# Expert search on VectorE: 2048-column sums and combinations in two pieces of 1024 columns

## What is computed

```python
def peer_ffn(h, w_q, sub1, sub2, u, v):
    qry = (h @ w_q).reshape(B, S, 8, 256)
    s1 = jnp.einsum('bshd,hkd->bshk', qry[..., :128], sub1)     # 128 keys a head
    s2 = jnp.einsum('bshd,hkd->bshk', qry[..., 128:], sub2)
    v1, i1 = lax.top_k(s1, 16)
    v2, i2 = lax.top_k(s2, 16)
    cand = (v1[..., :, None] + v2[..., None, :]).reshape(B, S, 8, 256)
    cand_idx = (i1[..., :, None] * 128 + i2[..., None, :]).reshape(B, S, 8, 256)
    top_s, pos = lax.top_k(cand, 16)
    expert = jnp.take_along_axis(cand_idx, pos, axis=-1)
    gate = jax.nn.softmax(top_s, axis=-1)
    a = jnp.einsum('cd,ced->ce', x_c, u[e_c])
    ...
    return jnp.einsum('ce,ced->cd', gelu(a) * gate, v[e_c])
```

## Time and profile before

| | |
|---|---|
| median of 3 runs | 1931.25 us (1930.73 to 1932.47) |
| the profiled execution | 1932.39 us, its span 1930.7 us |
| share of the span in which an engine is busy | PE 98%, DVE 78%, ACT 60%, POOL 12% |
| the search on VectorE | 209.78 to 314.24 us of the span |
| granted TensorE clock | 1.00 in every stretch read here (2.4 GHz) |

### The profile page before, as it was taken

How to read it: one execution, slowest core, us unless ns; L and a number is a source line. 1 busy time by engine, 2 the same in 40 slices (tenths; PEclk the granted TensorE clock), 3 DMA queues, 4 the chain that set the end, 5 groups by cost and what they waited for, 6 DMA issues and landing times.

```text
span 1930.7 us, 38686 instructions
## 1 busy us (share of the span) xinstructions
PE 1899.4 (98%) x12752; PEld 1728.6 (90%) x12752; DVE 1501.1 (78%) x3609; ACT 1157.9 (60%) x2442; POOL 233.6 (12%) x262
## 2 busy tenths in 40 slices
PE   9899999999999999999999999999999999999998
PEld 8779999999888899999989898998889989998886
DVE  6676798888778878888888487877887568887776
ACT  5645666998444444544466577655557567765555
POOL 1000695665000000000000000010000000010000
PEclk9999999999999999999999999999999999999999
DMA  8446555444775588777757533565665553455552
GB/s 309 153 171 236 179 174 169 139 150 137 255 254 192 198 312 288 280 281 291 263 206 262 197 131 121 171 212 191 248 246 177 186 175 121 139 179 175 185 191 103
DMA packets 109463, 388.33 MB, mean 201 GB/s; under 512 B 12160, under 2 KB 16528, under 8 KB 108304
## 3 DMA queue, kind: packets, MB, share of 16 engines
q1 hardware_dynamic: 95040, 335.40, 50.6%
q10 hardware_dynamic: 8096, 28.70, 4.3%
q0 software_dynamic: 6192, 22.55, 3.2%
HBM read 379.76 MB, written 6.82 MB: 200 GB/s over the span
## 4 chain that ended last, share of the span: by engine, by line
PE 86%; DVE 9%; ACT 2%; DVEq 2%; issue 1%; DMA 0%; ACTq 0%; SPq 0%
PE bank L763 13%; PE bank L771 12%; PE bank L768 12%; PE bank L1002 7%; PE bank L1008 7%; PE bank L1005 7%; PE bank L1405 5%; PE bank L1069 3%; PE bank L1402 2%; PE bank L901 1%; PE bank L1214 1%; DVE part_lo L2159 1%; PE bank L1263 1%; ACT part_hi L1473 1%; DVE arena L2388 1%
## 5 line engine op out<-in xcount | busy, mean ns | idle before, releaser
L1473 ACT ACTIVATE part_hi<-ring 128x512 fp32r<-128x512 f32 x1124 | 692.0, 626 | 369.8 <-PE bank L768 162.6
L2159 DVE TENSOR_TENSOR part_lo<-ring,part_hi 128x512 fp32r<-128x512 f32 (+1 forms) x764 | 507.6, 685 | 158.0 <-ACT part_hi L1473 148.8
L763 PE MATMUL bank<-u_hi,part_hi 128*128 128x256 f32 (+1 forms) x1888 | 545.2, 289 | 4.9 <-POOL part_lo L2061 3.4
L771 PE MATMUL bank<-u_hi,part_lo 128*128 128x256 f32 (+1 forms) x1888 | 529.8, 281 | 0.0
L768 PE MATMUL bank<-u_lo,part_hi 128*128 128x256 f32 x1808 | 505.8, 280 | 0.0
L763 PEld LDWEIGHTS bank<-u_hi,part_hi 128*128 128x128 f32 (+1 forms) x1888 | 354.7, 188 | 13.2 <-POOL part_lo L2061 4.6
L771 PEld LDWEIGHTS bank<-u_hi,part_lo 128*128 128x128 f32 (+1 forms) x1888 | 356.8, 189 | 0.0
L768 PEld LDWEIGHTS bank<-u_lo,part_hi 128*128 128x128 f32 x1808 | 339.7, 188 | 3.1
L1002 PE MATMUL bank<-part_hi,w_hi 128*128 128x512 f32 x688 | 269.1, 391 | 0.2 <-DVE w_lo L2488 0.2
L1008 PE MATMUL bank<-part_lo,w_hi 128*128 128x512 f32 x688 | 268.0, 389 | 0.0
L1005 PE MATMUL bank<-part_hi,w_lo 128*128 128x512 f32 x688 | 267.9, 389 | 0.0
(11 more groups left out here) (354 smaller groups left out, 3223.5 us busy)
## 6 DMA issues: line engine op xcount, KB each, us to landing
ring<-stream_dram SPq DMA_DIRECT2D x606, 512.0 KB, 3.3
arena<-ada_dram ACTq DMA_DIRECT2D x54, 512.0 KB, 4.7
arena<-ada_dram POOLq DMA_DIRECT2D x42, 512.0 KB, 4.5
acts_kept<-act SPq DMA_DIRECT2D x32, 128.0 KB, 3.6
arena<-acts_kept SPq DMA_DIRECT2D x4, 1024.0 KB, 5.4
xT<-x_dram SPq DMA_DIRECT2D x4, 256.0 KB, 5.4
arena<-mem_dram SPq DMA_DIRECT2D x1, 1024.0 KB, 9.1
arena<-keys_dram SPq DMA_DIRECT2D x1, 1024.0 KB, 8.2
```

The source lines that it names most:

```text
L763: m = pe.matmul(o, hi, u(cc), start=first, stop=False)
L771: m = pe.matmul(o, lo, u(cc), start=False, stop=last)
L1473: act.activation(part_hi[:, h % 4, 0:width], ring[:, n % RING, (h % 2) * width:(h % 2 + 1) * width], ACT.Copy).then_inc(hi_ready, 1)
L2159: v.tensor_tensor(part_lo[:, h % 4, 0:width], ring[:, n % RING, (h % 2) * width:(h % 2 + 1) * width], part_hi[:, h % 4, 0:width], ALU.subt ...
```

## The change

The sum into `cand` is made for heads 0 to 3 and then for heads 4 to 7, 1024 columns each. The combination into `apart` and the minimum behind it are made for the first four heads and then for the last four, so that the order on VectorE is combination, drain, minimum, combination, drain, minimum, drain for each side and tile. Nothing else is altered: the values, the buffers and the waits between engines stay.

```diff
-                v.tensor_tensor(cnd,
-                                topv[:, tt, 0:8, :].unsqueeze(3).to_broadcast([P, 8, 16, 16]),
-                                topv[:, tt, 8:16, :].unsqueeze(2).to_broadcast([P, 8, 16, 16]), ALU.add)
+                for h in (0, 4):
+                    v.tensor_tensor(cnd[:, h:h + 4, :, :],
+                                    topv[:, tt, h:h + 4, :].unsqueeze(3).to_broadcast([P, 4, 16, 16]),
+                                    topv[:, tt, 8 + h:12 + h, :].unsqueeze(2).to_broadcast([P, 4, 16, 16]), ALU.add)
...
                     at = at.bitcast(U32)[:, tt, :].rearrange("p (h k) -> p h k", h=8)
-                    v.tensor_tensor(apart_u.rearrange("p (h k a) -> p h k a", h=8, a=16),
-                                    at.unsqueeze(3).to_broadcast([P, 8, 16, 16]),
-                                    placed.bitcast(U32)[:, tt, side * 8:side * 8 + 8, :].unsqueeze(2)
-                                    .to_broadcast([P, 8, 16, 16]), ALU.bitwise_xor)
-                    v.drain()
-                    v.tensor_reduce(picks[:, side, tt, :], apart_u.rearrange("p (k a) -> p k a", a=16), AX_X, ALU.min)
+                    spread = apart_u.rearrange("p (h k a) -> p h k a", h=8, a=16)
+                    for h in (0, 4):
+                        v.tensor_tensor(spread[:, h:h + 4, :, :],
+                                        at[:, h:h + 4, :].unsqueeze(3).to_broadcast([P, 4, 16, 16]),
+                                        placed.bitcast(U32)[:, tt, side * 8 + h:side * 8 + h + 4, :].unsqueeze(2)
+                                        .to_broadcast([P, 4, 16, 16]), ALU.bitwise_xor)
+                        v.drain()
+                        v.tensor_reduce(picks[:, side, tt, h * 16:h * 16 + 64],
+                                        apart_u[:, h * 256:h * 256 + 1024].rearrange("p (k a) -> p k a", a=16),
+                                        AX_X, ALU.min)
                     v.drain()
```

## The result

| | before | changed |
|---|---|---|
| median of 8 runs each | 1931.55 us (1930.73 to 1932.47) | 1937.74 us (1936.70 to 1939.33) |
| ratio to before | | 1.0032, 95% interval 1.0021 to 1.0042 |
| the profiled execution, and its span | 1932.39, 1930.7 us | 1937.62, 1935.9 us |
| search on VectorE | 209.78 to 314.23 | 209.48 to 317.94 |
| start of the last L1069 matmul, the end of the dense stage | 478.52 | 483.51 |

The changed kernel is slower by 6.2 us. The forecast was 1935.2 us with a range of 1932.3 to 1936.9, so the result lies 0.8 us above the upper end of the range. Of the 2.5 us to the forecast, 0.3 are the median of the kernel before, which came out at 1931.55 and not at 1931.25.

A forecast was written before the change was run, and what follows sets the result against it. TensorE, 98% busy, bounds the kernel, and VectorE's end of the search decides when it resumes. First tile +3.57 and second +0.30 gave +3.87, taken as +3.95 us: median 1935.2 us, range 1932.3 to 1936.9.

The forecast's parts named there:

- what bounds the end: Behind the search TensorE has no idle time, so delay of VectorE's search end, 314.24, moves the end one for one.
- the fixed cost: On VectorE's list, two split sums at 0.08 and four split combinations with minima at 0.29 add 1.32 us.
- the waits, one by one: Walk through VectorE's waits for GpSimd's rests: with fixed cost, first tile 3.57 us later, second tile +0.30.
- The margin of 0.11 us: Next combination arrives 1.21 us behind the last one's end, GpSimd's second rest starts at 1.10, so it waits.
- rival (1): Rests fit under the minima, all eight combination waits zero, second sums still wait 1.08: +0.42 us, 1931.7 us; 12%.
- (2): Walk holds in kind but loses two or three first-tile waits: +1.3 to +3.3 us, 1932.6 to 1934.6; 14%.
- (3): Only two-port modes block; combinations keep their waits for another reason: +1.32 us, 1932.6 us; 2%.
- (4): GpSimd's last rest comes later than about 309.5, second tile's last three combinations wait: +7.9 at most, 1939.2; 14% over +4.7.
- (5): VectorE and GpSimd fall in step, all 8.87 us of waits go, TensorE gives back 3.9 us: 1927.4 us; 2%.
- the last one of the sum: Search ends at 318.2, TensorE resumes at 319.2 after standing since about 311.4; all behind moves by the same, +3.95 us.
- The sign: Whole kernel against the 0.2% line, 3.9 us: slower 48%, within it 50%, faster 2%.

The follow-up runs named there:

- the two quiet kernels: GpSimd's rests cut to 16 of 512 columns, in the kernel before and in the changed kernel; 1927.91 and 1927.47 us, one execution each.
- more_rests_pieces: Changed kernel with GpSimd making the rests of 37 experts instead of 34 and the gate's exponentials two experts later; median 1937.83 us against 1932.16 before.
- the third execution: The changed kernel once more, since an edit meant to add matmuls was void; median 1938.18 us against 1932.78 before.
- warm_filled: Changed kernel with TensorE's experts 30 to 35 written out and 56 unread matmuls before half 68; median 1936.61 us against 1932.16 before.
- sums_only: Kernel before with only the sums into `cand` in two pieces, combinations and minima whole; median 1934.91 us against 1932.78 before.
- quiet_whole: Kernel before with GpSimd's rests cut to 16 of 512 columns, other columns left out; 1927.91 us, one execution.
- quiet_pieces: Changed kernel with GpSimd's rests cut to 16 of 512 columns, other columns left out; 1927.47 us, one execution.
- comb_quarters: Kernel before with combinations and minima in four pieces of 512 columns, sums whole; 1938.67 us, one execution.

## Why the prediction was wrong by 2.5 us, point by point

**Right: what bounds the end.** The figure to forecast was the search's end, and a delay there was handed on to the end (the stages behind took only 0.24 us more). TensorE takes up half 68 at 0.98 us behind it in both kernels, and GpSimd's last rest, 4.9 us earlier, bought nothing.

**Right: the fixed cost.** 1.32 us by the sum, 1.36 us by the two quiet kernels.

**Right: the waits, one by one.** The second sum of each tile 1.08 and 1.09 (1.08 forecast), L2407 unchanged, the copy of the first tile 0 (0), the first tile's combinations 0.95, 1.05, 0.90, 1.06 (0.94, 1.04, 0.89, 1.04), the last three of the second tile 0 (0). The copy of the second tile waited 1.06 where 0.95 was forecast. GpSimd's last rest ran from 306.74 to 308.12 (306.9 to 308.3). The search grew by 4.01 us where +3.95 was forecast, and each half of the change gave its share, 1.18 and 2.82. The margin of 0.11 us is seen in a row: the second combination arrives at 253.66, 0.10 behind the start of the second rest at 253.56. At 512 columns it arrives under the first rest and waits 0.33. No run puts a combination just ahead of a rest, so what rival (1) would have given was not seen.

**The rivals.** (1) and (2), pieces that find the port free, fell: every combination that followed another one waited, in all kernels where GpSimd had work. (3), only two-port modes block, fell with the quiet kernels. The Trainium skill, "Advanced Engine Details and Errata", section "VectorE Performance Modes", names no other modes; the prediction's "by that page" is too wide, since it holds for this section and not for the whole page. The uint32 combination of 3.35 us that falls to 2.29 when GpSimd's rests are short speaks against the rule. (4), a late last rest, did not occur here, and more_rests_pieces shows what it would have cost the search: 7.0 us more than before, where the prediction had 7.9 at most for the time. (5), all waits gone, fell.

**The step that failed** is the last one of the sum: "TensorE resumes at 319.2, having stood since about 311.4, and all behind it moves by the same amount". The halt was forecast, from 311.4 to 319.2, and it came, from 311.35 to 318.92. What I did not read off my own forecast is that TensorE comes back from such a halt at half its clock. In the stretch that I read, its longest halt before was 1.27 us and the clock column read 1.00 throughout, so I took the pace behind the search, for given. The 7.57 us of halt brought it to 0.50, and the matmuls behind it cost 0.214 instead of 0.118 us, 17 of them in one execution, 28 in another kernel's. 17 x 0.096 is 1.6 us, of which the profiled execution gives 0.3 back, because a short wait of the kernel before (a matmul that starts at 318.36, 0.2 late, and the one behind it, 0.1 late) is gone; in the third execution 2.1 us remain. 4.0 + 1.3 to 2.1 is 5.3 to 6.1, and the medians are +6.2, +5.7 and +5.4. warm_filled takes that term away alone: with TensorE kept busy, the sum is again the forecast's (+4.05 in the trace, +4.45 by the medians). No row of before shows TensorE behind a halt of 7 us, so its cost was an unknown to be bounded: from nothing to half pace for as long as the halt, which is half of 7.6 us, would have put the upper end at 1935.2 + 3.8 = 1939.0 instead of 1936.9. That is a guess that would have served here and no rule: in sums_only the low stretch of the work, 6.1 us, was longer than the halt of 3.77.

**The sign.** My forecast lay on the 0.2% line, and the missing term decided: slower, for which I had 0.48.

## What to carry to other kernels

Where two engines hold each other up, as VectorE's combinations and GpSimd's rests did here, a cut instruction meets the other engine anew with each piece, as long as that one has work queued. What counted here was not the length of a piece but when the next one arrives: 1.21 us behind the end of the last one, when the second rest had begun at 1.10. Ask first who waits for the list: while TensorE waited for the end of the search the pieces cost 5 to 6 us, and with the hand-over moved so that it does not wait, the same pieces stand in the fastest whole kernel. And where a sum contains a halt of TensorE longer than those of the trace, it needs a second term, with a range, for the clock that it may come back with.

## What was unexpected of the hardware

From 200 to 345 us, halts of 1.27 us left the clock at 1.00 in the kernel before; halts of 2.28, 3.77, 5.75, 7.57 and 8.64 us were each followed, or met before their end, by a stretch at 0.50. But the length of the halt alone does not decide. The 3.20 us of more_rests_pieces left the clock at 1.00, and one and the same halt of 1.75 us, which ends near 73.7 us in every kernel, was followed by a low stretch of 3.4 us in four of the profiled executions (warm_filled, quiet_whole, quiet_pieces, comb_quarters) and by none in the ten others. The price does not grow with the halt: 28 matmuls at the low clock for the 3.77 us of sums_only, 17 for the 7.57 of the changed kernel. And it is not the same for one program: with equal halts the low stretch was 6.83 us in two executions and 10.24 in a third, of which TensorE's work met 3.6, 4.4 and 5.5 us. The Trainium skill, "TensorE: Matmul & The Clock Gate", section "Part 1: The HAM clock gate (the "warmup" mystery)", says that the number of slow matmuls varies from run to run of one kernel; these three executions agree (17, 20 and 25). The spread in "to grid", 165.57 to 166.42, is 0.85 us that no row of the kernel before foretells.
